# First modulation blocks by halves of their columns, and first products on half of the contraction rows

## The reference

```python
def modulated_norm(x, g, shift, scale):
    return rmsnorm(x, g) * (1 + scale) + shift

def swiglu(h, wg, wu, wd):
    return (jax.nn.silu(h @ wg) * (h @ wu)) @ wd

c_act = jax.nn.silu(c)
for l in range(DEPTH):
    mod = (c_act @ w_ada[l] + b_ada[l]).reshape(b, N_MOD, 1, D_MODEL)
    sh1, sc1, g1, sh2, sc2, g2, sh3, sc3, g3 = [mod[:, i] for i in range(N_MOD)]
    h = modulated_norm(x, norm_g[l, 0], sh1, sc1)
    x = x + 0.5 * g1 * swiglu(h, ffn_wg[l, 0], ffn_wu[l, 0], ffn_wd[l, 0])
    ...
```

## Time and profile before

| | before |
|---|---|
| median of 3 runs (lowest, highest) | 2397.67 us (2388.83, 2401.29) |
| profiled execution | 2392.03 us |
| its span | 2390.3 us |
| busy share PE / DVE / ACT / POOL | 97% / 70% / 47% / 13% |
| mean granted PE clock | 0.992 |
| HBM read | 474.52 MB, 199 GB/s over the span |

### The profile page before, as it was taken

How to read it: one execution, slowest core, us unless ns; L and a number is a source line. 1 busy time by engine, 2 the same in 40 slices (tenths; PEclk the granted TensorE clock), 3 DMA queues, 4 the chain that set the end, 5 groups by cost and what they waited for, 6 DMA issues and landing times.

```text
span 2390.3 us, 33494 instructions
## 1 busy us (share of the span) xinstructions
PE 2325.7 (97%) x13617; PEld 2005.7 (84%) x13617; DVE 1673.3 (70%) x1947; ACT 1129.3 (47%) x1398; POOL 319.3 (13%) x421
## 2 busy tenths in 40 slices
PE   5999989999999999999999999999999999999998
PEld 4787868887888988888889999888788899998887
DVE  6998557878886767656577886765655678858555
ACT  3444555445445455444455436454444465355442
POOL 3110201101113000010001830000100006500000
PEclk9999999999999999999999999999999999999999
DMA  9996329968984576555654334566556453444653
GB/s 332 359 335 244 128 87 310 314 220 292 317 314 160 178 229 219 178 181 192 211 164 115 115 118 153 182 200 223 160 193 214 144 158 98 144 133 159 203 194 123
DMA packets 336020, 477.76 MB, mean 200 GB/s; under 512 B 23068, under 2 KB 274299, under 8 KB 335867
## 3 DMA queue, kind: packets, MB, share of 16 engines
q1 hardware_dynamic: 313050, 396.33, 50.4%
q0 software_dynamic: 22816, 79.29, 9.2%
HBM read 474.52 MB, written 1.05 MB: 199 GB/s over the span
## 4 chain that ended last, share of the span: by engine, by line
PE 81%; DVE 6%; DMA 4%; ACT 3%; issue 3%; DVEq 2%; POOL 1%; SPq 0%; POOLq 0%; ACTq 0%
PE ps L970 19%; PE ps L972 19%; PE ps L971 19%; PE ps L1082 11%; PE ps L1084 6%; DMA raw<-in_ffn_wu_dram 2%; DVE w_lo L2390 2%; ACT w_hi L1891 1%; DVE mix_mem L2512 1%; DVEq L2528 1%; PE ps L1659 1%; PE ps L1045 1%; DMA raw<-in_ffn_w_up_dram 1%; DVE parts L2481 1%; POOL n_rstd L773 1%
## 5 line engine op out<-in xcount | busy, mean ns | idle before, releaser
L2390 DVE TENSOR_TENSOR w_lo<-raw,w_hi 128x2048 fp32r<-128x2048 f32 (+1 forms) x376 | 822.9, 2192 | 375.4 <-ACT w_hi L1891 370.8
L1891 ACT ACTIVATE w_hi<-raw 128x2048 fp32r<-128x2048 f32 (+2 forms) x368 | 687.4, 1868 | 554.1 <-DMA raw<-in_ffn_wu_dram 158.5
L1082 PE MATMUL ps<-x_both,w_hi 128*128 128x512 f32 x1120 | 397.3, 399 | 0.0
L970 PE MATMUL ps<-w_hi,x_both 128*128 128x512 f32 x944 | 377.2, 400 | 8.0 <-DVE x_both L2415 7.0
L972 PE MATMUL ps<-w_hi,x_both 128*128 128x512 f32 x944 | 370.0, 392 | 0.0
L971 PE MATMUL ps<-w_lo,x_both 128*128 128x512 f32 x944 | 369.3, 391 | 0.0
L1084 PE MATMUL ps<-x_both,w_lo 128*128 128x256 f32 x1120 | 314.5, 281 | 0.0
L970 PE MATMUL ps<-x_both,w_hi 128*128 128x256 f32 (+1 forms) x992 | 287.6, 290 | 0.5 <-ACT mix_mem L2294 0.4
L972 PE MATMUL ps<-x_both,w_lo 128*128 128x256 f32 (+1 forms) x992 | 282.2, 285 | 0.0
L971 PE MATMUL ps<-x_both,w_hi 128*128 128x256 f32 (+1 forms) x992 | 282.2, 284 | 0.0
L970 PE MATMUL ps<-w_hi,hid_hi 128*128 128x512 f32 x640 | 253.5, 396 | 5.0 <-DVE hid L2600 4.0
(11 more groups left out here) (430 smaller groups left out, 3253.2 us busy)
## 6 DMA issues: line engine op xcount, KB each, us to landing
raw<-in_w_in_dram SPq DMA_DIRECT2D x96, 512.0 KB, 4.6
raw<-in_ffn_wg_dram SPq DMA_DIRECT2D x88, 512.0 KB, 4.7
raw<-in_ffn_wu_dram SPq DMA_DIRECT2D x88, 512.0 KB, 6.0
raw<-in_ffn_w_gate_dram SPq DMA_DIRECT2D x88, 512.0 KB, 4.0
raw<-in_ffn_w_up_dram SPq DMA_DIRECT2D x88, 512.0 KB, 5.1
raw<-in_ffn_wd_dram SPq DMA_DIRECT2D x80, 512.0 KB, 5.3
raw<-in_ffn_w_down_dram SPq DMA_DIRECT2D x80, 512.0 KB, 4.1
spare<-in_w_ada_dram POOLq DMA_DIRECT2D x40, 512.0 KB, 5.9
```

What stands on the lines that cost most here:

```text
L970: pe.matmul(dst, wh, vh, start=start, stop=False, skip_group_check=True)
L1082: pe.matmul(both, h[:, i, col:col + P], x_both[:, :, k, :], start=(k == 0), stop=False, skip_group_check=True)
L1891: return f(w_hi[at.hi_slot()][:, cols], raw[at.raw_slot()][:, cols], ACT.Copy)
L2390: return v.tensor_tensor(w_lo[s][:, cols], raw[s][:, cols], w_hi[at.hi_slot()][:, cols].bitcast(F32), ALU.subtract)
```

## The change

**Modulation by halves of the columns.** A unit u is now half u // 8, row block u % 8: 512 columns of the shift and the same 512 of the scale (channels 0 to 511 in the first half, 512 to 1023 in the second), in two runs of 2 KB for each row. So after 8 units both shift and scale of channels 0 to 511 are known, told by a new semaphore `first_half_mod`.

**Four units on PE.** DVE takes units 0 to 11. Units 12 to 15 PE multiplies itself, with the unit as the stationary operand and one column of silu(c) as the moving one (`first_unit`, 8 products of one column), into the same PSUM columns as the second `first_sums`.

**Chunk order and first products.** The chunks of the first FFN come as (pair, half) = 0: (0,0), 1: (1,0), 2: (0,1), 3: (1,1). SP issues them when units 2, 7, 10 and 11 have landed. PE's order of blocks is (0,0,0), unit 13, (0,0,1), units 14 and 15, sums, (1,0,0), (0,1,0), (0,1,1), (1,1,0), transposes, (1,0,1), (1,1,1). Chunk 1 is thus finished after chunk 2; `freed(1) = 3` says so to SP and ACT. The six unread products are gone, and both tiles of x are transposed ahead of the first product.

```diff
+        def x_at(c, t, half):
+            return 2 * half + t + 1 if c == 0 else at_half(c, t, half)
+        ADA_BY_DVE = 12
+        def freed(n):
+            return 3 if n == 1 else n + 1
...
-                    sp.wait_ge(chunk_used, at.n - RAW_RING + 1)
+                    sp.wait_ge(chunk_used, freed(at.n - RAW_RING))
...
+                if c == 0:
+                    for u, (start, half) in ((2, (0, 0)), (7, (256, 0)), (10, (0, 1)), (11, (256, 1))):
+                        slot, turn = landing(0, u)
+                        sp.wait_ge(ada_landed[slot], turn * 16)
+                        load_gu(wg, wu, start, half)
+                    load(rows_of(wd, 0), 2)
+                for i in range(1 if c == 0 else 0, PAIRS - 2):
...
+                if f == 0:
+                    s0 = take()
+                    x_ready(0, 0, 0)
+                    gate_up(s0, 0, 0)
+                    first_unit(13)
+                    x_ready(0, 1, 0)
+                    used(gate_up(s0, 0, 1))
+                    first_unit(14)
+                    first_unit(15)
+                    first_sums(1)
+                    s2 = take()
+                    gate_up(s2, 0, 0, EARLY)
+                    s1 = take(1)
+                    x_ready(0, 0, 1)
+                    gate_up(s1, 1, 0).then_inc(gu_ready, 1)
+                    x_ready(0, 1, 1)
+                    gate_up(s1, 1, 1).then_inc(chunk_used, 1)
+                    s3 = take(2)
+                    gate_up(s3, 1, 0, EARLY).then_inc(gu_ready, 1)
+                    made(0, 0)
+                    made(0, 1)
+                    turn_hid((0, 1))
+                    gate_up(s2, 0, 1).then_inc(chunk_used, 1)
+                    gate_up(s3, 1, 1).then_inc(chunk_used, 1)
+                    at.n += 3
...
+            def first_unit(u):
+                slot, turn = landing(0, u)
+                k = u % KT
+                pe.wait_ge(ada_landed[slot], turn * 16)
+                if u == 15:
+                    pe.wait_ge(ada_used, ADA_BY_DVE)
+                for m in range(2):
+                    for t in range(4):
+                        col = KT * m + 4 + t
+                        at_ = 512 * m + t * P
+                        last = pe.matmul(ps[:, 3, col:col + 1], ada_raw[slot][:, at_:at_ + P], c_act[:, k:k + 1],
+                                         start=(u == ADA_BY_DVE and m == 0 and t == 0), stop=False, skip_group_check=True)
+                if u == 15:
+                    last.then_inc(ada_used, 16 - ADA_BY_DVE)
...
+            pe.wait_ge(c_ready, 1)
             first_sums(0)
             turn_x(0, 0, xn)
-
-            pe.wait_ge(ada_used, KT + 4)
-            for _ in range(6):
-                pe.matmul(ps[:, 3, :], ident[:], flat(vpad)[:, 0:512], start=True, stop=True)
-            first_sums(1)
+            turn_x(0, 1, xn)
+            first_unit(12)
             ffn(0, 0, xn, xn, 1)
...
-            modulated(0, 0)
+            modulated(0, 0, (0,))
+            modulated(0, 1, (0,))
             ahead(2)
+            modulated(0, 0, (1,))
+            ahead(3)
+            modulated(0, 1, (1,))
...
+            first_steps(range(KT))
             ahead(1)
-            x_lo_a(0, 0)
+            first_cols(0)
+            first_steps((8, 9))
+            x_lo_a(0, 0, (0,))
+            x_lo_a(0, 1, (0,))
+            first_steps((10, 11))
             ahead(2)
+            first_cols(1)
+            ahead(3)
+            x_lo_a(0, 0, (1,))
+            x_lo_a(0, 1, (1,))
```

More of the change, by code:

```diff
@@ L792, in _ @@
                     pool.wait_ge(ada_used, u - ADA_SLOTS + 1)
-                ada_unit(u // KT, u % KT, landing(0, u)[0])
+                slot, half, k = landing(0, u)[0], u // KT, u % KT
+                both = a["w_ada"][0].rearrange("(k p) n -> p k n", p=P)[:, k, 0:2 * D].rearrange("p (m n) -> p m n", m=2)
+                pool.dma_start(ada_raw[slot].rearrange("p (m n) -> p m n", m=2), both[:, :, 512 * half:512 * half + 512])\
+                    .then_inc(ada_landed[slot], 16)
                 if u == 10:
@@ L1298, in _, with first_sums @@
             pe.transpose(ps[:, 0, 256:328], b_rows[:, 1, :], ident[0:72, 0:72]).then_inc(rows_turned, 1)
[L1300 to L1304, removed]
[L1305 removed]
+            def first_sums(half):
+                pe.wait_ge(ada_used, KT if half == 0 else ADA_BY_DVE)
+                for m in range(2):
+                    for t in range(4):
+                        col = KT * m + 4 * half + t
+                        at_ = 512 * m + t * P
+                        last = pe.matmul(ps[:, 2 + half, col:col + 1], ada_acc[:, half, at_:at_ + P], ones[:, 0:1],
+                                         start=(half == 0 and m == 0 and t == 0), stop=True, skip_group_check=True)
+                last.then_inc(cols_summed, 1)
+            def first_unit(u):
[4 more added lines that the diff above has]
+                    pe.wait_ge(ada_used, ADA_BY_DVE)
+                for m in range(2):
+                    for t in range(4):
+                        col = KT * m + 4 + t
+                        at_ = 512 * m + t * P
+                        last = pe.matmul(ps[:, 3, col:col + 1], ada_raw[slot][:, at_:at_ + P], c_act[:, k:k + 1],
[3 more added lines that the diff above has]
+            pe.wait_ge(c_ready, 1)
             first_sums(0)
             turn_x(0, 0, xn)
[L1310 to L1313 removed]
+            turn_x(0, 1, xn)
+            first_unit(12)
             ffn(0, 0, xn, xn, 1)
@@ L1929, in turned_x, with modulated @@
                 return ps[:, 4 + 2 * t + half, :].rearrange("p (k n) -> p k n", k=4)
-            def modulated(c, t):
-                act.wait_ge(mod_ready, mod_group(c) + 1)
-                for half in range(2):
+            def modulated(c, t, halves=(0, 1)):
+                if halves == (0,):
+                    act.wait_ge(first_half_mod, 1)
+                else:
+                    act.wait_ge(mod_ready, mod_group(c) + 1)
+                for half in halves:
                     act.wait_ge(xt_done, at_half(c, t, half))
```

107 lines of the change are left out of this document (56 added, 51 removed).

## The result

After the change the median is 2414.01 us (2410.84 to 2416.64, 5 runs), before it 2397.67 us (2388.83 to 2401.29, 5 runs). The ratio is 1.0081 with a 95% interval of 1.0063 to 1.0099: slower by 0.8%. The profiled execution took 2412.81 us, its span is 2411.0, 20.7 us above the span before. The forecast was 2406 with a range of 2397 to 2416; so the time lies in the range and on the slow side, but I had called "within 0.5%" likeliest, and the loss is 16.3 us by the medians and 20.7 by the spans where the sum said 10.

What follows compares the result with a forecast made beforehand. PE, busy 97% of the span, was taken as the bound. The first down product for tile 0 comes 8.1 us later plus 2 for the clock, about +10 on the runs' mean of 2395.9: 2406 us, range 2397 to 2416.

Steps and rivals of the forecast that it cites:

- the row: Start of the first down product for tile 0 on PE, 71.42 before; forecast at 79.5, +8.1 us.
- Chunk 0's landing: Ahead of the first product: chunk 0's second half, issued at about 12.6, lands 10.9 us later, at 23.5.
- Units and sums, taken as fast: PE's one-column work after the first product: 1.84 us a unit, not 3.57, so column sums end at 47.5.
- The second half in series: Behind the column sums, bias, modulations, chunk 2's conversion and splits run serially on ACT and DVE, from 47.5 to 55.9.
- `tables()`: DVE's piece behind the second half's splits: 4.4 us that nothing covers any more, bringing 55.9 to 60.3.
- The load of chunk 6: Issued only when chunk 1's place is released at 68.8; the load takes 6.05 us, ahead of conversion and made.
- The clock: Two PE idle times of 4.5 to 4.7 us may restart PE at 1.2 GHz: 0 to 3.0 us, taken as 2.
- New idle time behind 90 us: Sign against the forecast: PE shows new idle time, or makes time up, behind 90 us, where nothing is changed.
- (a): Rival: the early start carries through and the first down product comes up to 7 us sooner, 2389 us; chance 0.07.
- (b): Rival: PE's clock falls during one-column products, the next block starts slow; +12 to +18, 2408 to 2414; chance 0.25.
- (c): Rival: little contention and fast units, +3 to +7, 2399 to 2403 us; chance 0.18.
- The rule on queues: DMA queues take turns packet by packet; by it blocks 4 to 7 take about 2.0 us, the sum 1 us more.

Runs made afterwards that it cites:

- e4: Changed kernel with chunk 0 issued straight behind x, without the wait for the third block; 2408.15 us, ratio 1.0063.
- e7: Kernel before with chunk 0 issued when the third block has landed instead of when ten are used; 2395.44 us, ratio 1.0008.
- e1: Changed kernel with ACT's and DVE's conversions of chunks 2 and 3 moved ahead of the second half's columns; 2406.67 us, ratio 1.0066.
- e2: e1 with the old chunk order and the old release of chunk 1's ring place; 2401.94 us, ratio 1.0030.
- e6: Changed kernel with tables() on DVE moved ahead of the second half's bias; 2415.37 us, ratio 1.0081.
- e3: Changed kernel with all 16 units on DVE and none on PE; 2406.36 us, ratio 1.0073.
- e9: Changed kernel with silu (ACT) and made (DVE) ahead of chunk 6's conversion in pair 1 of the first FFN; 2411.38 us, ratio 1.0074.
- e11: e8 with the second half's bias ahead of chunk 3's conversion and tables() behind the split; 2393.16 us, ratio 0.9995.
- e10: Kernel before with the edit of e9 alone; 2390.13 us, ratio 0.9987.
- e5: Changed kernel with 23 products added whose result nobody reads, in three places where PE waits; 2418.33 us, ratio 1.0096.
- e8: Changed kernel: all units on DVE, old chunk order and release, chunk 0 straight behind x, conversions and tables() ahead of second half's columns; 2402.01 us, ratio 1.0026.

## Why the prediction was right and wrong

Its frame held: nearly all of the loss is made between the start and the row, nothing behind 90 us gives it back, the row comes late because chunk 6 is issued late, and an early first product buys nothing. Its milestones, forecast against measured, and the same in e4, where chunk 0 lands early:

| milestone | forecast | measured | late so far | e4 |
|---|---|---|---|---|
| 8th block ends | 21.7 | 20.9 | -0.8 | 23.3 |
| first product | 32.8 | 37.89 | 5.1 | 33.53 |
| column sums end | 47.5 | 52.9 | 5.4 | 51.5 |
| chunk 1 released | 68.8 | 75.45 | 6.7 | 75.95 |
| the row | 79.5 | 88.05 | 8.6 | 87.22 |

Of the 8.6 us, 5.1 were there at the first product, 0.3 came up to the sums, 1.3 between the sums and the release, and 1.9 with chunk 6's load.

- **Chunk 0's landing** is the first step that failed. I took 10.9 us from issue to landing out of a stretch where the blocks were nearly done, and 17.0 were measured (e7: 16.5, e4: 16.8). I had put the price of contention on the blocks (1.71 us each); they ran on almost unhindered, 1.49 us each from the third to the eighth, and chunk 0 paid. So the first product was bound by chunk 0's conversion and DVE's work behind it (29.64 to 37.89 on the chain), not by PE's one-column stages, which ended at 30.45.
- **Units and sums, taken as fast,** are the second. In the changed kernel they fit: 37.89 to 52.9 is 15.0 us against 14.7 in the sum, units took 1.84 to 1.93, only the last sums were slower (2.59). But that size does not hold for a kernel in which chunk 0 lands about as forecast (21.1 against 23.5). That kernel is e4: its first product is 0.7 us off the forecast, its sums 4.0, its row 7.7. So the late landing explains when the first product came, and is not by itself what made the row late.
- **The second half in series** was the right mechanism, and e1 and e2 show its parts (6.9 and 3.8 us at the row). One term was missing in it: ACT's 1.9 us for chunk 3 (64.99 on the chain), which lengthened the stretch by 1.3. For `tables()` the stretch from the split to `made(0,0)` had the right size by luck (61.2 to 65.26, 4.1 us against 4.4): PE's slow block and `silu(0,0)` take as long beside it, and without `tables()` the row stayed (e6).
- **The load of chunk 6** was taken as 6.05 us and took 7.98 from 75.45 to 83.43. Its down weights, which had waited with it, were issued right behind it (75.45 and 76.42). In the six runs in which they were (the changed kernel, e1, e3, e4, e6, e9), its second half landed 6.2 to 8.4 us after issue; in e2 and e11, where they followed 5.9 us later, 5.0.
- **The clock** was put at 2 us, 0 to 3. The row's own block took 4.82 us (88.05 to 92.87) where a fast one takes 2.75, 2.1 us. The block at 60.25 was slow for the most part, but `tables()` ran beside it to 65.1.
- Row and restart make 18.6 us by 92.87, and the wait at 139.47 adds 1.5. "New idle time behind 90 us" was on my list of what would prove me wrong: I had not looked past the row for the next piece of work, pair 2 and later, that was late as well (e9 and e10 meet it too). Of the signs that were to show the forecast, none fell in its bracket; the wait ahead of block (pair 0, half 1) was 2.07 us where I had 4 to 5.
- **Rivals.** (a) did not happen, for the reason given: the sums ended at 52.9 and not by 38.9 (71.42 less 32 is 39.4). (b) gave the right size, 12 to 18, by luck: the clock did fall in the last sums (granted 0.72 from 50.30 to 52.70) and the block behind was slow (0.50), as it had it, but that cost 0.75 us in the sums, and the block is not on the chain. It is real all the same: in e4 and e5 it took back what a sooner or faster start had given. (c) is out. The rule on queues fits one stretch of the trace (e7), and its price fell on chunk 0 and not on the blocks.
- The chances put 0.61 on "within 0.5%" because the sum ended at 10 us, just below 12. With chunk 0 at 17 us the same working gives about 15 and the slow side. That the range held the time is owed to the room left for (b).

## What to carry to other kernels

A load that is issued earlier beside a full queue takes longer: in e7, 10.9 us of earlier issue brought it in 5.4 us earlier (28.84 against 34.24), and in e4, where it landed 8.5 us before the changed kernel's, the eighth block ended 2.4 us later. Look up what share of the bytes its packets get there, and don't take its duration from a stretch in which the other queue runs dry. And don't count on an early milestone alone: in e4 a first product 4.4 us sooner brought the row 0.8 us. When the first input of a phase is split so that the phase can start sooner, list what stands behind the last piece: the conversions, releases and loads that used to run beside the long wait are now in series, and each must be moved to where its engine idles (e1, e2), in the order in which its result is needed (e8 against e11). A wait named for one producer can be a matter of queue order: ask what the waiting instruction truly needs (e9, e10).

## What the runs showed that I had not expected

Two runs of 2 KB instead of one of 4 KB left POOL's packets as large as they were: 3.65 KB in the changed kernel, 3.67 in e7.

The granted clock can fall in the middle of work, some products behind a wait. After the idle time of 2.07 us ahead of 60.25, PE's timeline in the changed kernel begins fast (0.23 us from product to product, 2.4 GHz) and turns slow (0.43, 1.2 GHz) five products later; the granted clock is 1.00 from 60.25 to 61.50 and 0.50 from 62.00 to 64.50:

```profile
60.25 0.47 PE L987 MATMUL ps<-w_hi,x_both 128*128 128x512 f32 x1 [2.07 <-DVE x_both L2486]
60.55 0.39 PE L988 MATMUL ps<-w_lo,x_both 128*128 128x512 f32 x1
...
61.48 0.53 PE L989 MATMUL ps<-w_hi,x_both 128*128 128x512 f32 x1
61.81 0.63 PE L987 MATMUL ps<-w_hi,x_both 128*128 128x512 f32 x1
```

What PE did before: units and sums of one column, a block at 1.2 GHz (0.43 us a product), the wait. The sums at 50.27 took 2.59 us there, 1.95 in e3 without units on PE, and 3.55 in e4 and e5. What exactly in one-column work lets the clock fall no run here separates. Nor is one-column work needed for it: in e6, 24 products of 128x512 ran at 2.4 GHz (granted 1.00 from 60.90 to 66.30), PE waited 1.89 us, and the block at 68.41 began fast and went on at 0.50 (70.00 to 72.80); e5 has the same behind the same wait at 69.83. In e2 a wait of 2.20 us ahead of the row was not followed by it (1.00 from 77.40 to 79.50).
